# Two stacked transformer blocks in fp32 pairs: feed-forwards 2 to 4 with another split of the second product, other banks for two units, and two plain products

## Chip, cores and metric

One core of one Trainium2 chip runs the whole kernel. The metric is the device time of one execution in microseconds (us). All inputs and outputs are fp32. The kernel has four feed-forwards (FF), one in each of its four layers; the change touches the last three of them.

## The reference, cut to what matters

```python
# first block, layers 0 and 1
h = rmsnorm(x, norm_ffn_g[l]) * (1.0 + sc2) + sh2
f = (jax.nn.silu(h @ ffn_w1[l]) * (h @ ffn_w3[l])) @ ffn_w2[l]
x = x + g2 * f
...
# second block, layers 0 and 1
gate, up = jnp.split(x @ w_ffn_in[i], 2, axis=-1)
ffn = (jax.nn.silu(gate) * up) @ w_ffn_out[i]
ple = (p[i] @ w_ple[i]) * jax.nn.sigmoid(x @ w_ple_gate[i])
x = layer_norm(ALPHA * x + ffn + ple, ln2_g[i], ln2_b[i])
```

There are 512 tokens of width 1024, and the hidden width is 2816. Attention, pooling, retention, convolution and gating stand ahead of each feed-forward and are not changed.

## The kernel before

**Number format.** Each fp32 operand is split into a high part (fp32r, made by ACT) and a low part (the rest, `raw - hi`, made by POOL or DVE). One product is three matmuls: high by low, low by high, high by high (`three`, lines 2789 to 2791).

**Pairs, units, parts.** The hidden width is 11 pairs of 2 x 128 columns. A unit is one load of weights with the products that use it. The order is written out by the class `Plan`: for each pair i one unit of the up side (`plain` or `upper`; w3, or the second half of w_ffn_in) and one of the gate side (`seven`, or `whole` for pair 0 of a feed-forward of the first block), then some `down` units. A `plain` unit has 4 parts of 12 matmuls of 512 columns. A `seven` or `upper` unit computes the same 256 hidden columns in the seven products of a Strassen-Winograd scheme: 7 parts M1, M6, M7, M5, M4, M2, M3, each of 12 matmuls of 256 columns. It needs four sums of weight quarters (`dve_sums`, lines 2062 to 2067, tile `u_sum`) and five operations on DVE that add up the results (`parts` in `dve_ffn`, lines 2095 to 2112). Every part has a slot in a ring of 8 (`k_hi`, `k_lo`). A slot is filled again when PE has done the part that held it, and the fill is three steps: ACT's high part (line 1097), the low part (line 1654 on POOL or 2047 on DVE), PE.

**Down units.** The second product (w2) is summed in PSUM over a pass of pairs and then added to x. `SPREAD` gives the passes of feed-forwards 2 to 4: pairs 0-1, 2-3, 4-5, 6-7, 8-10. Each pass has four `down` units of 256 output columns. The units of the first four passes lie between the pairs; those of the last pass are the tail, units 38 to 41. A down unit has one part of 12 matmuls of 512 columns for each pair of its pass.

**The gate.** When both units of a pair are done, ACT takes the silu (line 1121), DVE multiplies with the up side (`gated`, line 2125, tile `u_full`), ACT makes `f_hi` (line 1126) and POOL (line 1674) or DVE (line 2133) makes `f_lo`. PE takes a bank again when its reader is done (`bank_taken`); for the bank of a `plain` unit that reader is `gated`.

**Order on the engines.** All queues are in order. ACT, POOL and DVE walk through the same list of parts `t` as PE. `Plan.after[t]` says which slots are filled behind part t; `Plan.summed` says ahead of which part DVE makes the sums of a later unit. SP issues the loads in the order of the units; a load waits for the low parts of the unit that used the buffer before. In the first block SP also loads pieces of the modulation matrix (`sp_modulation_b`), and DVE weighs them (lines 1895 and 1898, tile `r`).

**The end of a feed-forward in the second block.** When the first half of unit 40 is done, PE sums x over the first four of its eight column blocks with a matmul by ones (line 3629); DVE then subtracts, adds and squares (`dve_shift_norm`, lines 2484 to 2498), and PE takes up those sums (lines 3346 and 3348) ahead of the last six matmuls of unit 41.

Of the kernel before, what the change touches and what calls it, by code (L numbers as in the profile page):

```python
# [36 lines left out]
DEPTH = 2  # L37
# [17 lines left out]

PAIRS = FF // G
PASSES = [range(0, 4), range(4, 7), range(7, PAIRS)]
SPREAD = [range(0, 2), range(2, 4), range(4, 6), range(6, 8), range(8, PAIRS)]
AHEAD = [0, 1, 0]
SPARE = 5  # L60
RING = 8
# [5 lines left out]
class Plan:  # L67
# [8 lines left out]
    def __init__(self, early, spread, uppers=(), sets=(1,)):  # L76
        self.units, self.spread, self.sets = [], spread, sets
        self.early, self.spare = early, SPARE - 1 if spread else SPARE
        self.passes = SPREAD if spread else PASSES
        downs = [("down", n, j) for n in range(len(self.passes)) for j in range(KD // 2)]  # L80
        upto = {pairs[-1] + AHEAD[n]: KD // 2 for n, pairs in enumerate(PASSES)}
        if spread:
            upto = {i: 4 if early and i == 3 else 2 for i in range(3 if early else 2, PAIRS - 1)}
        for i in range(PAIRS):
            self.units += [("upper" if i in uppers else "plain", i, 0),
                           ("whole" if early and i == 0 else "seven", i, 0)]
            self.units += downs[:upto.get(i, 0)]
            del downs[:upto.get(i, 0)]
        self.units += downs
        self.tail = len(self.units) - KD // 2  # L90
        self.seq = [(u, n) for u in range(len(self.units)) for n in range(self.count(u))]
        self.at = {x: q for q, x in enumerate(self.seq)}
        self.slot, self.before, holds = [], [], {}
        for q, (u, n) in enumerate(self.seq):
            k = LAST_SLOTS[u - self.tail][n] if u >= self.tail else q % RING
            self.slot.append(k)
            self.before.append(holds.get(k, -1))
            holds[k] = q
        self.after, at = {t: [] for t in range(len(self.seq))}, 0
        for q in range(RING, len(self.seq)):  # L100
            at = max(at, self.before[q])
            self.after[at].append(q)
        self.mine = [self.on_vector(u, n) for u, n in self.seq]
        self.summed = {}
        for u, (kind, _, _) in enumerate(self.units):
            if kind in SEVENS and self.at[u, M6] >= RING:
                t = next(t for t, qs in self.after.items() if self.at[u, M6] in qs)
                self.summed[t - (3 if spread and (kind == "upper" or len(sets) > 1) else 1)] = u
        self.source, self.loads, self.old, used = [], [], [], {}
        for u in range(len(self.units)):  # L110
            x = self.buffer(u)
            self.source.append(x)
            self.loads.append(sum(y == x for y in self.source))
            self.old.append(used.get(x))
            used[x] = u
# [17 lines left out]
    def banks(self, u):  # L133
        kind, i, j = self.units[u]
        if kind == "seven":
            return 0, 4, 1, 5
        if kind == "upper":
            return 2, 6, 3, 7
        if kind == "whole":
            first = 0  # L140
        elif kind == "plain":
            late = i > 0 and (i != 2 or not self.early)
            first = 6 if (late if self.spread else (i % 2 == 1) != (i >= len(PASSES[0]))) else 2
        else:
            first = 2 * (u % 2) if not self.spread or u >= self.tail else 0 if j % 2 else 2
        return first, first + 1

    def pair_units(self, i):
# [23 lines left out]
        return self.mine[q], sum(m == self.mine[q] for m in self.mine[:q + 1])  # L172


PLAN = [Plan(True, False), Plan(True, True, range(4, PAIRS))] + [Plan(False, True, range(1, PAIRS), (2, 1))] * DEPTH
UNITS = {1: 10 + 4, 2: 9 + 4 + 5}
UNIT0 = {1: 0, 2: DEPTH * UNITS[1]}

# [286 lines left out]
class Sems:  # L465

    def __init__(self, nc, ctx):
# [89 lines left out]
        def by_plan(name, count):  # L557
            return FfnSignal(ctx.enter_context(nc.semaphore(name)), [count(p) for p in PLAN])

# [327 lines left out]
def sp_layer1(sp, e, l, more):  # L887
    a, b, s = e.a, e.b, e.s
    lay = Layer(s, 1, l)

    def units(js):
        for j in js:
            sp_weights(sp, e, lay, j, a["w_in"], l, IN1[UNIT_COLS1[j]])

    if l == 0:
        units((2, 3))
        sp.wait_ge(*s.mod(l, 1))
        sp_gains(sp, e, (0, 1, 2, 3))
        units((4,))
        sp_gains(sp, e, (4, 5))  # L900
        units((5,))
        sp_gains(sp, e, (6, 7))
        sp.wait_ge(s.z_ready.up, 9 + Z_COPIES)
    else:
        sp_after_ffn(sp, e, l - 1)
        units((0, 1))
        sp.wait_ge(*s.f_x(l - 1, KD * len(PLAN[l - 1].passes)))
        sp.wait_ge(*s.r(l * 2, 2))
    sp.dma_start(b.decay[:, :, :], a["decay"]).then_inc(s.decay_in.up, 16)
    for m in range(2):  # L910
        sp.dma_start(b.pw[:, m, :], a["pool_w"][l, 2 * m:2 * m + 2, :, :].rearrange("e c d -> (e c) d"))\
          .then_inc(s.decay_in.up, 16)
    units(range(6 if l == 0 else 2, 10))
    for j in range(4):
        sp_weights(sp, e, lay, 10 + j, a["w_out"], l, G * j)
    sp.wait_ge(*s.gn_o(l, 2))
    for n in range(4):
        sp_modulation_b(sp, e, l, n)
    ffn = a["ffn_w1"], a["ffn_w3"], 0, a["ffn_w2"], l
    for u in range(2):  # L920
        sp_ffn_unit(sp, e, lay, u, *ffn)
    sp.wait_ge(*s.hl(l * 2 + 1, 1))
    for n in (4, 5):
        sp_modulation_b(sp, e, l, n)

    def between(u):
        if u in (4, 6):
            sp_modulation_b(sp, e, l, 6 + (u - 4) // 2)
        if u == 8 and lay.plan.spread:
            sp.wait_ge(*s.b_acc(l, 3 * KD + KD // 2))  # L930
        if more and 10 <= u < 10 + A_CHUNKS:
            sp_next_modulation(sp, e, l, u - 10)

    sp_ffn(sp, e, lay, *ffn, 2, between)
    if more:
        sp_parameters(sp, e, l + 1)
# [730 lines left out]
def pool_ffn(pool, e, lay):  # L1667
    s, b, plan, n = e.s, e.b, lay.plan, lay.ffn

    def hidden(i):  # L1670
        for m in range(2):
            at = i % plan.spare * 2 + m
            pool.wait_ge(*s.fh(n, 2 * i + m + 1))
            pool.tensor_tensor(b.f_lo[:, at, :], b.f_full[:, m, :], b.f_hi[:, at, :].bitcast(F32), ALU.subtract)\
                .then_inc(s.fl.up, 1)

    for t, (u, part) in enumerate(plan.seq):
        if part == 1 and plan.gate_done(u) is not None and not plan.hidden_on_vector(u):
            hidden(plan.gate_done(u))
        for q in plan.after[t]:  # L1680
            pool_low(pool, e, lay, q)
# [2024 lines left out]
```

## Time and profile before

| | before |
|---|---|
| median of 3 runs | 2558.11 us (2552.84 to 2560.55) |
| the profiled execution | 2559.09 us |
| its span in the profile | 2557.3 us |
| mean granted TensorE clock | 0.979 of full speed |
| feed-forwards 2, 3, 4 in the span | about 895 to 1234, 1527 to 1884, 2177 to 2533 us |

The profile shows one execution. Its span lacks 1.8 us that lie around it. Times in the rows are from the start of the span; "PE" is TensorE, "DVE" VectorE, "ACT" ScalarE, "POOL" GpSimd.

### The profile page before, as it was taken

Reading aid. Unit: us, or ns where it says so; the run is one execution under the profiler, and the core shown is the slowest. Engines: PE = TensorE matmul, PEld = TensorE weight load, DVE = VectorE, ACT = ScalarE, POOL = GpSimd, SP = SyncE. Lnnn points to the kernel's source line nnn. Section 1 sums busy time; section 2 is a strip of 40 time slices with the busy share of each in tenths; the row PEclk is TensorE's granted clock in tenths of the full one; section 3 lists DMA queues with packets and bytes.
Section 4 is the critical chain, followed back from the end, with each engine's and each line's share of the span. In section 5 each row is a group of like instructions: output and inputs, shape, how many; then the busy total and the mean of one; then the engine's idle time right before and its main releaser. Section 6 shows DMA issues by size and latency. Waiting matters only on the chain.

```text
span 2557.3 us, 35757 instructions
## 1 busy us (share of the span) xinstructions
PE 2442.4 (96%) x13831; PEld 2055.3 (80%) x13831; DVE 1841.5 (72%) x2737; ACT 1109.2 (43%) x1827; POOL 1080.9 (42%) x606
## 2 busy tenths in 40 slices
PE   7999999999999999999899998999989999899997
PEld 4776788888776788998677778999967777899995
DVE  5686777854487796776686477888668747888876
ACT  4335443323425443444443554444444355444442
POOL 0332462524324353545153456445514534655541
PEclk8999999999999999999999999999999999999998
DMA  8514346543222433332331223333223212333321
GB/s 281 199 50 132 116 142 193 188 137 101 85 82 83 132 116 116 100 107 76 100 83 58 67 66 108 108 99 100 83 80 83 75 50 66 99 104 112 107 79 46
DMA packets 239650, 268.92 MB, mean 105 GB/s; under 512 B 19977, under 2 KB 204025, under 8 KB 239225
## 3 DMA queue, kind: packets, MB, share of 16 engines
q1 hardware_dynamic: 239480, 266.63, 32.3%
q8 instruction: 110, 1.80, 0.3%
q14 instruction: 60, 0.48, 0.1%
HBM read 264.51 MB, written 2.10 MB: 104 GB/s over the span
## 4 chain that ended last, share of the span: by engine, by line
PE 74%; DVE 11%; issue 4%; ACT 4%; DMA 3%; POOL 3%; SPq 0%; ACTq 0%; DVEq 0%; POOLq 0%
PE bank L2789 22%; PE bank L2791 22%; PE bank L2790 22%; DVE r L1898 2%; DVE m_cv L2239 2%; POOL w_lo L1643 1%; DMA raw<-in_ffn_w 1%; DVE k_lo L2047 1%; POOL k_lo L1654 1%; DMA raw<-in_w_ffn_in 1%; PE bank L3423 1%; DMA b_raw<-in_ada_w 1%; ACT w_hi L1043 1%; ACT k_hi L1097 1%; PE bank L3456 1%
## 5 line engine op out<-in xcount | busy, mean ns | idle before, releaser
L1654 POOL TENSOR_TENSOR k_lo<-raw,k_hi 128x512 fp32r<-128x512 f32 x303 | 440.3, 1462 | 569.4 <-ACT k_hi L1097 568.6
L1643 POOL TENSOR_TENSOR w_lo<-raw,w_hi 128x2048 fp32r<-128x2048 f32 x53 | 248.5, 4688 | 532.4 <-ACT w_hi L1043 457.5
L1097 ACT ACTIVATE k_hi<-raw 128x512 fp32r<-128x512 f32 x432 | 265.0, 626 | 310.3 <-PE bank L2791 244.1
L2789 PE MATMUL bank<-h_hi,k_lo 128*128 128x256 f32 (+1 forms) x1132 | 355.6, 314 | 17.4 <-DVE u_full L2125 13.7
L2790 PE MATMUL bank<-h_lo,k_hi 128*128 128x256 f32 (+1 forms) x1132 | 354.2, 313 | 0.0
L2791 PE MATMUL bank<-h_hi,k_hi 128*128 128x256 f32 (+1 forms) x1132 | 354.1, 313 | 0.0
L2789 PE MATMUL bank<-h_hi,w_lo 128*128 128x512 f32 x800 | 325.2, 406 | 8.6 <-DVE h_lo L2007 3.9
L2791 PE MATMUL bank<-h_hi,w_hi 128*128 128x512 f32 x800 | 314.0, 393 | 0.0
L2790 PE MATMUL bank<-h_lo,w_hi 128*128 128x512 f32 x800 | 313.7, 392 | 0.0
L2791 PE MATMUL bank<-u_t_hi,k_hi 128*128 128x256 f32 x1104 | 310.9, 282 | 0.0
L2789 PE MATMUL bank<-u_t_hi,k_lo 128*128 128x256 f32 x1104 | 310.3, 281 | 0.0
L2790 PE MATMUL bank<-u_t_lo,k_hi 128*128 128x256 f32 x1104 | 307.9, 279 | 0.0
L2789 PE MATMUL bank<-f_hi,k_lo 128*128 128x512 f32 x704 | 279.7, 397 | 10.5 <-DVE x L2393 4.5
L2790 PE MATMUL bank<-f_lo,k_hi 128*128 128x512 f32 x704 | 275.8, 392 | 0.0
L2791 PE MATMUL bank<-f_hi,k_hi 128*128 128x512 f32 x704 | 275.5, 391 | 0.0
L2789 PEld LDWEIGHTS bank<-h_hi,k_lo 128*128 128x128 f32 x1132 | 216.9, 192 | 32.8 <-DVE u_full L2125 14.1
L2790 PEld LDWEIGHTS bank<-h_lo,k_hi 128*128 128x128 f32 x1132 | 217.3, 192 | 12.5
L2791 PEld LDWEIGHTS bank<-h_hi,k_hi 128*128 128x128 f32 x1132 | 217.3, 192 | 12.0
L1097 ACT ACTIVATE k_hi<-u_sum 128x512 fp32r<-128x512 f32 x207 | 129.9, 628 | 184.4 <-PE bank L2791 123.0
L2789 PEld LDWEIGHTS bank<-u_t_hi,k_lo 128*128 128x128 f32 x1104 | 209.0, 189 | 0.0
L2790 PEld LDWEIGHTS bank<-u_t_lo,k_hi 128*128 128x128 f32 x1104 | 208.8, 189 | 0.0
L2791 PEld LDWEIGHTS bank<-u_t_hi,k_hi 128*128 128x128 f32 x1104 | 208.0, 188 | 0.0
(401 smaller groups left out, 5013.0 us busy)
## 6 DMA issues: line engine op xcount, KB each, us to landing
raw<-in_ffn_w SPq DMA_DIRECT2D x52, 1024.0 KB, 5.4
raw<-in_w_ffn_in SPq DMA_DIRECT2D x44, 1024.0 KB, 5.1
raw<-in_w_in SPq DMA_DIRECT2D x34, 1024.0 KB
b_raw<-in_ada_w SPq DMA_DIRECT2D x32, 1024.0 KB, 5.2
f_raw<-in_w_ffn_out SPq DMA_DIRECT2D x32, 512.0 KB, 3.4
z_a<-in_ada_w SPq DMA_DIRECT2D x4, 2048.0 KB, 14.1
g_raw<-in_ada_w SPq DMA_DIRECT2D x8, 1024.0 KB, 5.4
raw<-in_w_out SPq DMA_DIRECT2D x8, 1024.0 KB
```

The costliest lines, as they stand in the source:

```text
L1043: act.activation(b.w_hi[p][:, 0:n], b.raw[p][:, 0:n], ACT.Copy).then_inc(s.hi.up, 1)
L1097: act.activation(hi, src, ACT.Copy).then_inc(s.f_hi.up, 1)
L1643: pool.tensor_tensor(b.w_lo[p][:, 0:n], b.raw[p][:, 0:n], b.w_hi[p][:, 0:n].bitcast(F32), ALU.subtract)\
L1654: pool.tensor_tensor(lo, src, hi.bitcast(F32), ALU.subtract).then_inc(s.f_lo.up, 1)
L1898: dve.scalar_tensor_tensor(acc, raw[:, k - ks[0], :], c[:, k:k + 1], acc, ALU.mult, ALU.add)\
L2047: dve.tensor_tensor(lo, src, hi.bitcast(F32), ALU.subtract).then_inc(s.f_lod.up, 1)
L2239: dve.scalar_tensor_tensor(b.cv[:, m, :], b.ch[:, m, t:t + T], b.taps[:, n:n + 1], b.cv[:, m, :], ALU.mult, ALU.add).then_inc(s.conv.up, 1)
L2789: pe.matmul(out, wlo, xhi, start=start, stop=False)
L2790: pe.matmul(out, whi, xlo, start=False, stop=False)
L2791: return pe.matmul(out, whi, xhi, start=False, stop=stop)
L3423: op = pe.matmul(bank[at][:, c:c + n], b.n_q[o:o + HD, p, i * P:(i + 1) * P], b.n_k[o:o + HD, p // 2, 0:n], start=False, stop=(h, i) in (( ...
L3456: op = pe.matmul(bank[5][HD * h:HD * (h + 1), j * P:T], b.n_v[:, j, v], b.n_probT[h][:, KEY_AT[j]:KEY_AT[j] + T - j * P], start=(j == 0), ...
```

## The change

`SPREAD` becomes passes of 2, 2, 2, 1 and 4 pairs: pair 7 moves from the fourth pass to the tail. Units 30, 31, 34 and 35 have one part in place of two, units 38 to 41 have four in place of three. The up side of pairs 9 and 10 is a `plain` unit (2 units in each of three feed-forwards). In feed-forwards 3 and 4 the first unit, which is plain, writes banks 3 and 7 in place of 2 and 3; in feed-forward 2 the third down unit (unit 10) writes banks 6 and 7 in place of 2 and 3. In feed-forwards 3 and 4 DVE makes the sums of units 3 and 5 three parts later. In feed-forward 2 SP issues the last modulation piece behind the load of unit 7 in place of unit 6. POOL makes `f_lo` at a down unit's only part where it has just one.

```diff
-SPREAD = [range(0, 2), range(2, 4), range(4, 6), range(6, 8), range(8, PAIRS)]
+SPREAD = [range(0, 2), range(2, 4), range(4, 6), range(6, 7), range(7, PAIRS)]
...
-                self.summed[t - (3 if spread and (kind == "upper" or len(sets) > 1) else 1)] = u
+                ahead = 3 if spread and (kind == "upper" or len(sets) > 1) else 1
+                if len(sets) > 1 and kind == "seven" and self.units[u - 2][0] == "seven":
+                    ahead = 0
+                self.summed[t - ahead] = u
...
+            if self.spread and self.early and i == 0 and j == 2:
+                first = 6
+        if kind == "plain" and self.spread and not self.early and i == 0:
+            return 3, 7
         return first, first + 1
...
-PLAN = [Plan(True, False), Plan(True, True, range(4, PAIRS))] + [Plan(False, True, range(1, PAIRS), (2, 1))] * DEPTH
+PLAN = [Plan(True, False), Plan(True, True, range(4, 9))] + [Plan(False, True, range(1, 9), (2, 1))] * DEPTH
...
-        if u in (4, 6):
+        if u in (4, 7 if lay.plan.spread else 6):
...
-        if part == 1 and plan.gate_done(u) is not None and not plan.hidden_on_vector(u):
+        if part == min(1, plan.count(u) - 1) and plan.gate_done(u) is not None and not plan.hidden_on_vector(u):
```

The file of the change has seven lines more, so line 2062 of before is line 2069 of the change, and so on.

**DVE at the start of feed-forward 3**, before, from part M4 of unit 1 on; `u_act<-u_third,bank` to `u_act<-u_row,bank` are that unit's results, `u_sum_116` to `118` the sums of unit 3:

```order
L2105 TENSOR_TENSOR u_act<-u_third,bank 128x512
L2108 TENSOR_TENSOR u_row<-u_row,bank 128x256
L2062 TENSOR_TENSOR u_sum_116<-raw_53 128x512
L2064 TENSOR_TENSOR u_sum_117<-u_sum_116,raw_53 128x512
L2065 TENSOR_TENSOR raw_53<-raw_53 128x4x128
L2067 TENSOR_TENSOR u_sum_118<-raw_53,u_sum_117 128x512
L2047 TENSOR_TENSOR k_lo<-raw_52,k_hi 128x512
L2112 TENSOR_TENSOR u_act<-u_row,bank 128x512
L2047 TENSOR_TENSOR k_lo<-u_sum_108,k_hi 128x512
L2125 TENSOR_TENSOR u_full<-u_act,bank 128x512 x2
```

and the same place in the change:

```order
L2112 TENSOR_TENSOR u_act<-u_third,bank 128x512
L2115 TENSOR_TENSOR u_row<-u_row,bank 128x256
L2054 TENSOR_TENSOR k_lo<-raw_52,k_hi 128x512
L2119 TENSOR_TENSOR u_act<-u_row,bank 128x512
L2054 TENSOR_TENSOR k_lo<-u_sum_108,k_hi 128x512
L2132 TENSOR_TENSOR u_full<-u_act,bank 128x512 x2
L2069 TENSOR_TENSOR u_sum_116<-raw_53 128x512
L2071 TENSOR_TENSOR u_sum_117<-u_sum_116,raw_53 128x512
L2072 TENSOR_TENSOR raw_53<-raw_53 128x4x128
L2074 TENSOR_TENSOR u_sum_118<-raw_53,u_sum_117 128x512
```

The four sums of unit 3 stood ahead of the last result of unit 1 and of the gate of pair 0; now they stand behind them.

**PE at the same place**, before: the end of unit 1 (bank 5) and the beginning of unit 2. `f_gated` is the signal of the gate's multiplication:

```order
L2789 MATMUL bank5<-h_hi_50,k_lo_120 128x256
L2790 MATMUL bank5<-h_lo_51,k_hi_119 128x256
L2791 MATMUL bank5<-h_hi_50,k_hi_119 128x256
L2789 MATMUL bank2<-h_hi_50,k_lo_120 128x256 [waits f_lo,f_gated]
L2790 MATMUL bank2<-h_lo_51,k_hi_119 128x256
```

and the place in unit 2 where the change first waits for that signal, from part M7 (bank 6) to part M5 (bank 3):

```order
L2797 MATMUL bank6<-u_t_lo_115,k_hi_119 128x256
L2798 MATMUL bank6<-u_t_hi_113,k_hi_119 128x256
L2796 MATMUL bank3<-u_t_hi_113,k_lo_120 128x256 [waits f_lod,f_gated]
L2797 MATMUL bank3<-u_t_lo_115,k_hi_119 128x256
L2798 MATMUL bank3<-u_t_hi_113,k_hi_119 128x256
```

The wait for the gate of pair 0 moved from the first part of unit 2 to its fourth, 36 matmuls later.

**ACT at the end of feed-forward 2**, before, from the first sum of unit 37 (`u_row<-bank`) on; `raw_52` and `raw_53` hold the weights of units 38 and 39, and the second `u_act` is the silu that the gate of pair 10 waits for:

```order
L1116 ACTIVATE u_row<-bank 128x256
L1097 ACTIVATE k_hi<-raw_52 128x512
L1121 ACTIVATE u_act<-u_act 128x512
L1097 ACTIVATE k_hi<-raw_52 128x512 x2
L1097 ACTIVATE k_hi<-raw_53 128x512 x3
L1121 ACTIVATE u_act<-u_act 128x512
L1126 ACTIVATE f_hi<-u_full 128x512 x2
```

and in the change:

```order
L1123 ACTIVATE u_row<-bank 128x256
L1128 ACTIVATE u_act<-u_act 128x512
L1104 ACTIVATE k_hi<-raw_52 128x512 x4
L1104 ACTIVATE k_hi<-raw_53 128x512 x4
L1128 ACTIVATE u_act<-u_act 128x512
L1133 ACTIVATE f_hi<-u_full 128x512 x2
```

In the change all eight high parts of units 38 and 39 stand behind the end of unit 37: the first slot of unit 38 is the slot of unit 37's last part (both are slot 0 in the ring of 8), and `after` never lets a later slot be filled ahead of an earlier one. In feed-forwards 3 and 4 the slots fall otherwise: units 37's last part holds slot 4, and the four high parts of unit 38 lie ahead of its end, those of unit 39 behind it.

## Rows read from the trace of the kernel before

**Rows 1.** The page, parts 1 and 5: busy time by engine; the largest group on POOL

```profile
PE 2442.4 (96%) x13831; PEld 2055.3 (80%) x13831; DVE 1841.5 (72%) x2737; ACT 1109.2 (43%) x1827; POOL 1080.9 (42%) x606
...
L1654 POOL TENSOR_TENSOR k_lo<-raw,k_hi 128x512 fp32r<-128x512 f32 x303 | 440.3, 1462 | 569.4 <-ACT k_hi L1097 568.6
```

**Rows 2.** Timeline of PE, feed-forward 2: starts of units 12, 13, 14, 16

```profile
991.89 0.28 PE L2789 MATMUL bank<-h_hi,k_lo 128*128 128x256 f32 x1
...
1001.86 0.28 PE L2789 MATMUL bank<-h_hi,k_lo 128*128 128x256 f32 x1
...
1011.83 0.40 PE L2789 MATMUL bank<-f_hi,k_lo 128*128 128x512 f32 x1
...
1022.74 0.28 PE L2789 MATMUL bank<-h_hi,k_lo 128*128 128x256 f32 x1
```

**Rows 3.** Timeline of PE and DVE around the start of unit 10, feed-forward 2

```profile
974.51 0.39 PE L2791 MATMUL bank<-f_hi,k_hi 128*128 128x512 f32 x1
979.40 0.76 PE L2789 MATMUL bank<-f_hi,k_lo 128*128 128x512 f32 x1 [4.50 <-DVE x L2393]
...
971.91 0.69 DVE L2062 TENSOR_TENSOR u_sum<-raw 128x512 f32<-128x512 f32 x1 [3.91 <-DMA raw<-in_ffn_w]
...
975.90 1.29 DVE L2125 TENSOR_TENSOR u_full<-u_act,bank 128x512 f32<-128x512 f32 x2 [0.76 <-ACT u_act L1121]
...
977.89 1.41 DVE L2393 SCALAR_TENSOR_TENSOR x<-bank,mod,x 128x512 f32<-128x512 f32 x2
```

**Rows 4.** Timeline of PE and ACT, unit 38 of feed-forward 2; last, feed-forward 1

```profile
1202.15 0.39 PE L2791 MATMUL bank<-f_hi,k_hi 128*128 128x512 f32 x1
1205.05 0.77 PE L2789 MATMUL bank<-f_hi,k_lo 128*128 128x512 f32 x1 [2.50 <-DVE f_lo L2133]
...
1197.11 2.20 ACT L1097 ACTIVATE k_hi<-raw 128x512 fp32r<-128x512 f32 x4 [0.81 <-PE bank L2791]
...
362.85 0.47 PE L2789 MATMUL bank<-f_hi,k_lo 128*128 128x512 f32 x1 [2.43 <-DVE u_row L2108]
```

**Rows 5.** Timeline of four engines, start of feed-forward 3

```profile
1547.94 0.28 PE L2791 MATMUL bank<-h_hi,k_hi 128*128 128x256 f32 x1
1555.37 0.58 PE L2789 MATMUL bank<-h_hi,k_lo 128*128 128x256 f32 x1 [7.15 <-DVE u_full L2125]
...
1567.21 0.28 PE L2789 MATMUL bank<-h_hi,k_lo 128*128 128x256 f32 x1
...
1549.10 0.63 ACT L1097 ACTIVATE k_hi<-raw 128x512 fp32r<-128x512 f32 x1 [1.65 <-DMA raw<-in_w_ffn_in]
...
1553.25 0.68 DVE L2112 TENSOR_TENSOR u_act<-u_row,bank 128x512 f32<-128x512 f32 x1
...
1554.63 1.28 DVE L2125 TENSOR_TENSOR u_full<-u_act,bank 128x512 f32<-128x512 f32 x2
...
1566.51 1.66 DVE L2064 TENSOR_TENSOR u_sum<-u_sum,raw 128x512 f32<-128x512 f32 x1
...
1561.32 3.35 POOL L1674 TENSOR_TENSOR f_lo<-u_full,f_hi 128x512 fp32r<-128x512 f32 x2 [9.73 <-ACT f_hi L1126]
```

**Rows 6.** Timeline of PE, start of feed-forward 4

```profile
2197.72 0.28 PE L2791 MATMUL bank<-h_hi,k_hi 128*128 128x256 f32 x1
2204.53 0.58 PE L2789 MATMUL bank<-h_hi,k_lo 128*128 128x256 f32 x1 [6.54 <-DVE u_full L2125]
```

**Rows 7.** Timeline of PE and DVE, tail of feed-forward 3

```profile
1864.33 1.02 PE L3629 MATMUL bank<-r,ones 128*128 128x512 f32 x2
...
1879.23 1.13 PE L3346 MATMUL bank<-r,ones 128*128 128x512 f32 x2 [2.96 <-DVE r L2493]
...
1883.97 0.40 PE L2791 MATMUL bank<-f_hi,k_hi 128*128 128x512 f32 x1
...
1865.38 4.87 DVE L2498 SCALAR_TENSOR_TENSOR x<-bank,x 128x512 f32<-128x512 f32 x8 [2.39 <-PE bank L3629]
...
1878.48 0.69 DVE L2493 TENSOR_TENSOR r<-r,x 128x512 f32<-128x512 f32 x1
```

## The prediction

> **What bounds the kernel now.** The page comes first: PE is busy for 96% of the span, DVE for 72%, POOL for 42% [rows 1]. So PE's own work, and what keeps PE waiting, set the time; work on another engine counts only where PE waits for it. The second view is the timeline of PE through feed-forwards 2 to 4. Between the pairs it has no holes: a `seven` or `upper` unit of 84 matmuls takes 1001.86 - 991.89 = 9.97 us, and 48 matmuls of 512 columns take 1022.74 - 1011.83 = 10.91 us, 0.227 us each [rows 2]. So an 84-matmul unit has parts of 1.42 us, a down or plain part takes 2.73 us, and a `plain` unit 10.91 us. Third come the places where PE does stop. In these three feed-forwards there are six that matter, in four kinds:
>
> (a) Feed-forward 2, unit 10. PE ends unit 9 at 974.51 + 0.23 = 974.74 and starts again at 979.40, 4.66 us later, when DVE has emptied banks 2 and 3 (977.89 + 1.41 = 979.30). DVE is late because it stood 3.91 us for a load and then had sums and a gate to do [rows 3]. The first matmul afterwards takes 0.76 us, not 0.39: the granted clock is at 1.2 GHz, its lower level. The 48 matmuls up to 991.89 [rows 2] take 12.49 us, 1.6 more than 10.91. Loss 6.3 us.
>
> (b) Feed-forward 2, unit 38. After 24 matmuls PE waits for `f_lo` of pair 10: 1205.05 - 1202.38 = 2.67 us, and again the clock falls (0.77 us) [rows 4]; with the same 1.6 us the loss is 4.3 us.
>
> (c) Feed-forwards 3 and 4, unit 2. It wants bank 2, which the plain unit 0 left full until the gate of pair 0. In feed-forward 3 that is 1555.37 - 1548.06 = 7.31 us, and the unit's 84 matmuls then take 1567.21 - 1555.37 = 11.84 us, 1.87 more than 9.97 [rows 2, 5]. Loss 9.2 us. In feed-forward 4: 2204.53 - 2197.84 = 6.69 us [rows 6], with the same 1.87 us 8.6 us.
>
> (d) The tails of feed-forwards 3 and 4. From the half of unit 40 (1864.33) to the end of unit 41 (1883.97 + 0.23) 19.87 us pass. PE has 54 matmuls to do there, 12.26 us, and three matmuls by ones at no more than 1.02 us each, 3.06. The loss is 4.6 us: PE waits until 1879.23 for DVE's sum `r`, and DVE works from 1865.38 on without a rest [rows 7]. I take the same for feed-forward 4.
>
> **The change, part by part.**
>
> *Plain units for pairs 9 and 10.* Six units go from 9.97 to 10.91 us of PE: 0.94 x 6 = 5.6 us more, 1.9 in each feed-forward. PE is the bound between the pairs, so nothing hides this. DVE and POOL lose work there (four sums, five results, three low parts a unit), which earns nothing by itself.
>
> *Pair 7 to the tail.* PE's work is the same; four units lose 12 matmuls and four gain them. What it buys is cover. In (d), DVE has `r` ready at 1878.48 + 0.69 = 1879.17, 14.84 us after the half of unit 40 [rows 7]. The change gives PE 24 + 24 + 18 = 66 matmuls there ahead of the sums, 14.98 us, and one matmul by ones: 15.8 to 16.0 us. That covers DVE by about 1 us, and the squares come one short DVE operation later, behind another matmul by ones. So the 4.6 us go, in each of two feed-forwards. The least it can give is 3.1: the 12 extra matmuls of unit 41 and a little.
> In (b) PE gets 36 matmuls (8.2 us) in place of 24 ahead of pair 10. But the order of ACT in the change shows a new hole: unit 38 can't get its first slot before unit 37 has ended. ACT's high part (0.55, a quarter of 2.20 [rows 4]), POOL's low part (1.46 [rows 1]) and the hand-overs (0.2 before ACT, as in [rows 4]) give 2.3 us of idle PE. Eight high parts in place of four put off the silu by 2.2 us, so `f_lo` comes at 1205.0 + 2.2 = 1207.2, 10.3 us after unit 37's end (1196.9), while PE wants it at 2.3 + 8.2 = 10.5. No second wait. Loss 2.3 in place of 4.3 if the clock holds: gain 2.0. The clock is the unknown: after 2.43 us of idle it held (0.47 us), after 2.50 it fell (0.77) [rows 4]. At 2.3 I take it as holding; the other end is a gain of 0.4.
>
> *Unit 10 in banks 6 and 7.* It must wait for the gate of pair 3 instead, which is done at 975.90 + 1.29 = 977.19, not 979.30 [rows 3]: gain 2.1 us. The idle time falls from 4.50 to 2.4, nearest to the row where the clock held, so I add the 1.6 us: 3.7. The other end is 2.1. What is late next is the gate itself, behind the load that lands for DVE at 971.91; unit 12 takes banks 2 and 6 far later.
>
> *The first plain unit in banks 3 and 7, sums later.* Unit 2 wants bank 3 first at its fourth part, 4.27 us after it starts, at 1552.3. The gate of pair 0 was at 1554.63 + 1.28 because DVE had done the four sums of unit 3 first and only then the last result of unit 1 (1553.25) [rows 5]. With the sums behind, DVE has that result by 1549. ACT still stands at the high part of unit 3 for a load, until 1549.10 + 0.63 = 1549.73 [rows 5]; the silu ends at 1550.4, the two products at 1551.7. That is ahead of 1552.3, so the hole of (c) goes: 9.2 and 8.6 us. PE then runs 9 us earlier against DVE, and something else can be late. Sums of unit 3: 1551.7 to 1554.4 or so, wanted by PE at 1548.06 + 9.97 + 1.42 = 1559.5; fine. Next, DVE's result of M4 of unit 2 waits for `f_lo` of pair 0; ACT makes the high parts by about 1556, POOL needs 3.35 us [rows 5], so 1559.3; only then come the sums of unit 4 (2.7 us at 0.68 each, 4.7 if half of them take 1.66 [rows 5]), and the low part of M2 of unit 3 at 1562.7 to 1565. PE wants it at 1565.1. Pair 2 repeats this with the moved sums of unit 5. I put 1.8 us of new waits on each feed-forward; the ends are 0 and 4.
>
> By the Trainium skill (SBUF — State Buffer, SBUF: two separate sides), a DVE operation with two SBUF inputs and a GpSimd operation that reads SBUF exclude each other for a whole instruction. The sum at 1566.51, 1.66 us in place of 0.68, agrees. By that rule all four sums behind the gate could take 1.66, 6.6 us, which would put the low part of M2 at 1566.6 and add some 1.5 us a feed-forward: this is part of the second rival.
>
> *The modulation piece.* SP's load of unit 7 waits for low parts anyway, the piece is weighed some 20 us later, and `f_lo` of pair 9 at a one-part unit costs the same. I cost these at nothing; if the piece came late, DVE would hold up the emptying of banks, at most the few us of (a) again.
>
> **The sum.** Feed-forward 2: 3.7 + 2.0 - 1.9 = 3.8. Feed-forward 3: 9.2 - 1.8 + 4.6 - 1.9 = 10.1. Feed-forward 4: 8.6 - 1.8 + 4.6 - 1.9 = 9.5. Together 23.4 us off 2559.1, the profiled execution's own time (1 us above the median of the runs shown): 2535.7, say 2536 us.
>
> **The rivals.**
> *DVE becomes the bound at the starts (0.18).* For it: the moved sums meet POOL's `f_lo` and low parts, and DVE has 9 us less time. Against it: the slack of 4 us at unit 3's sums worked out above. Each of feed-forwards 3 and 4 then keeps 3 to 5 us of the hole, with 1.87 us of slow clock if it is one long wait: 10 us less gain, 2546 us.
> *The tails give nothing (0.06).* If DVE's chain there hangs on something later than the half of unit 40, for instance on ACT with two more high parts a unit, it shifts with PE. For it: DVE rests between units 38 and 40. Against it: its start at 1865.38 is released by PE's line 3629 [rows 7]. 2536 + 9 = 2545 us.
> *The bank changes don't do what they say (0.05).* If a load, not a bank, sets (a) and (c), only 4.27 us of (c) are covered by the three parts moved ahead: 2559.1 less 2 x (4.27 - 1.9 + 4.6) - 1.9 gives 2547 us.
> *Slower (0.04).* The sums of units 3 and 5 stand behind the gate. If they came so late that PE waited at the second part of those units, each us late costs PE a us, twice. It decides at 11.7 us late in each of two feed-forwards, that is sums of unit 3 ready only near 1571; at 15.6 us late the time is 2567 us. Only a load of unit 3 or POOL far behind could do it, and the load lands at 1549.
> *The forecast (0.67)* holds 2531 to 2541: 2531 with no new waits at all, 2541 with the clock falling at both places and 3 us of new waits in each start.
>
> **Range and chances.** A difference of 0.3% (7.7 us) is about what a measurement of this kernel tells from no change. Faster by more takes all cases down to 2550: 0.93. Same 0.04, slower 0.03. The range of 8 in 10 reaches from just under the best case, 2529, to the rivals at 2546 to 2547: 2529 to 2547.
>
> **What would show it.** In the profile after: unit 2 of feed-forwards 3 and 4 starts within 0.2 us of unit 1's end, and DVE's `u_full` product stands ahead of the sums from `raw`; PE's wait for `r` at line 3353 is gone; unit 10 starts some 2 us earlier; PE has a hole of 2.3 us for `k_lo` at the start of unit 38 in feed-forward 2. I would be wrong if PE showed new waits for `k_lo` on DVE in pairs 1 and 2, or if units 32 to 37 had holes because loads come too late for the shorter pairs.

## The result, and the profile after

The change makes the kernel 1.1% faster. Its median is 2528.71 us (2523.63 to 2535.36, 4 runs) against 2556.59 us for the kernel before (4 runs): a ratio of 0.9892 [0.9864, 0.9921]. Two later measurements of the same change gave 0.9887 [0.9874, 0.9901] and 0.9902 [0.9886, 0.9919]. The forecast was 2536, in a range from 2529 to 2547: the time fell just under its lower end, and the gain is some 25 to 28 us where 23.4 were worked out.

The busy times of the page, which answer to [rows 1]:

```profile
PE 2440.2 (96%) x13615; PEld 2044.6 (81%) x13615; DVE 1771.5 (70%) x2671; ACT 1094.8 (43%) x1803; POOL 1067.2 (42%) x600
```

PE's busy time is nearly what it was: the saving is idle time. The view of windows puts it in its place. Each row is a stretch, its length, and the busy us of PE, PEld, DVE, ACT and POOL, then the granted clock and the DMA. Of before, feed-forwards 2 and 3 (the first window begins 1.9 us behind the start of its feed-forward):

```profile
877.70:1234.40 356.70, 348.60 (x2207) 316.03 (x2206) 265.64 (x350) 153.86 (x262) 164.80 (x104) 0.99 0.35 109
1527.20:1884.20 357.00, 346.89 (x2347) 320.98 (x2345) 280.20 (x376) 157.89 (x268) 179.79 (x117) 0.99 0.31 97
```

and of after:

```profile
875.80:1233.80 358.00, 352.05 (x2140) 315.52 (x2141) 249.37 (x330) 151.56 (x256) 160.25 (x102) 0.99 0.34 109
1525.60:1871.00 345.40, 344.65 (x2274) 316.58 (x2274) 255.47 (x354) 152.27 (x260) 174.24 (x115) 1.00 0.32 101
```

In feed-forward 3 PE is now idle for 0.75 us in all, where it was 10.1, with the clock at full, and feed-forward 4 is the same; feed-forward 2 has gained nothing. Counted from the start of the first to the start of the last matmul of a feed-forward, in us (the kernels e2 to e13 are described under Experiments):

| kernel | FF2 | FF3 | FF4 |
|---|---|---|---|
| before, three profiled executions | 357.6, 357.7, 356.5 | 356.8, 356.8, 356.8 | 355.7, 356.1, 356.1 |
| the change, three | 358.0, 356.6, 358.5 | 345.4, 345.7, 345.5 | 345.4, 345.2, 345.2 |
| e2_passes | 353.4 | 359.7 | 358.8 |
| e3_starts | 356.7 | 349.3 | 350.0 |
| e5_banks37 | 357.7 | 351.2 | 353.1 |
| e6_sums | 356.6 | 350.5 | 350.6 |
| e4_uppers | 349.7 | 350.5 | 350.0 |
| e13_upper_banks | 351.5 | 347.7 | 345.4 |
| e10_ff2_upper | 352.5 | 345.2 | 346.5 |
| e12_nine_upper | 349.6 | 344.5 | 344.3 |

The three feed-forwards are 21.6 us shorter on the mean of three runs each (1070.1 against 1048.5).

**The starts of feed-forwards 3 and 4.** PE and DVE in feed-forward 3, which answer to [rows 5]:

```profile
1547.81 0.28 PE L2798 MATMUL bank<-h_hi,k_hi 128*128 128x256 f32 x1
1547.93 0.28 PE L2796 MATMUL bank<-u_t_hi,k_lo 128*128 128x256 f32 x1
...
1579.15 0.28 PE L2798 MATMUL bank<-u_t_hi,k_hi 128*128 128x256 f32 x1
1580.18 0.36 PE L2796 MATMUL bank<-u_t_hi,k_lo 128*128 128x256 f32 x1 [0.75 <-POOL k_lo L1661]
```
```profile
1548.65 1.28 DVE L2132 TENSOR_TENSOR u_full<-u_act,bank 128x512 f32<-128x512 f32 x2 [0.67 <-ACT u_act L1128]
1549.85 0.68 DVE L2069 TENSOR_TENSOR u_sum<-raw 128x512 f32<-128x512 f32 x1
...
1558.11 1.67 DVE L2071 TENSOR_TENSOR u_sum<-u_sum,raw 128x512 f32<-128x512 f32 x1
```

Unit 2 follows unit 1 without a gap; the gate stands ahead of the sums and starts 6.0 us earlier than before, of which 1.6 are the earlier start of the whole feed-forward. One new wait is left, 0.9 us for a low part of POOL (1580.18 less 1579.15 and the usual 0.12).

**The tails.** PE, which answers to [rows 7]:

```profile
1852.28 1.02 PE L3636 MATMUL bank<-r,ones 128*128 128x512 f32 x2
...
1868.15 1.02 PE L3353 MATMUL bank<-r,ones 128*128 128x512 f32 x2
...
1871.02 0.40 PE L2798 MATMUL bank<-f_hi,k_hi 128*128 128x512 f32 x1
```
```profile
1866.44 0.69 DVE L2500 TENSOR_TENSOR r<-r,x 128x512 f32<-128x512 f32 x1
```

From the half of unit 40 to the end 1871.25 - 1852.28 = 18.97 us pass, for 72 matmuls (16.34) and the ones; before it was 19.87 for 54. The time beyond the 512-column matmuls of the products is 7.61 us before and 2.63 us now, so the loss is 4.98 us less. DVE has `r` ready at 1867.13, 1.0 us before PE asks: the cover that was forecast ("about 1 us").

**Feed-forward 2, units 10 and 38.** PE, which answers to [rows 3, 4]:

```profile
974.45 0.39 PE L2798 MATMUL bank<-f_hi,k_hi 128*128 128x512 f32 x1
977.26 0.47 PE L2796 MATMUL bank<-f_hi,k_lo 128*128 128x512 f32 x1 [2.42 <-DVE u_full L2132]
...
978.43 0.63 PE L2797 MATMUL bank<-f_lo,k_hi 128*128 128x512 f32 x1
978.86 0.63 PE L2798 MATMUL bank<-f_hi,k_hi 128*128 128x512 f32 x1
...
1186.18 0.28 PE L2798 MATMUL bank<-h_hi,k_hi 128*128 128x256 f32 x1
1188.73 0.47 PE L2796 MATMUL bank<-f_hi,k_lo 128*128 128x512 f32 x1 [2.27 <-POOL k_lo L1661]
...
1190.19 0.63 PE L2798 MATMUL bank<-f_hi,k_hi 128*128 128x512 f32 x1
```

In this execution both holes have the length that was worked out (2.4 and 2.3 us of idle PE). The one at unit 38 has it in all three profiled executions of the change; the one at unit 10 was longer in the two others (by the starts 2.85 and 3.54 us, where it is 2.58 here). But look at the rows behind the holes: 1.2 and 1.5 us after PE starts again a matmul takes 0.63 us in place of 0.39, and the next comes 0.43 us later in place of 0.23. The granted clock fell to 1.2 GHz after both holes, where it was taken as holding. That the first matmul behind a hole takes only 0.47 us, which the prediction read as a clock that holds, is no sign of it here. And this feed-forward also pays 1.9 us for its two plain units (2 x 0.94): its matmuls without holes and slow stretches take 347.1 us, before 345.3.

### The profile page after: what moved, and what is told of

It reads as the page before. It is cut to its first block, busy times and chain, and to the rows that moved or that the text cites. A ratio compares the mean times of both kernels' runs of the same rounds, so it can differ in the third digit from the quotient of the medians.

```text
span 2533.6 us, 35157 instructions
## 1 busy us (share of the span) xinstructions
PE 2440.2 (96%) x13615; PEld 2044.6 (81%) x13615; DVE 1771.5 (70%) x2671; ACT 1094.8 (43%) x1803; POOL 1067.2 (42%) x600
## 4 chain that ended last, share of the span: by engine, by line
PE 71%; DVE 12%; issue 5%; ACT 4%; POOL 4%; DMA 3%; SPq 0%; ACTq 0%; DVEq 0%; POOLq 0%
PE bank L2796 21%; PE bank L2798 21%; PE bank L2797 21%; DVE r L1905 2%; DVE m_cv L2246 2%; DVE k_lo L2054 1%; DMA raw<-in_ffn_w 1%; DMA raw<-in_w_ffn_in 1%; POOL w_lo L1650 1%; POOL k_lo L1661 1%; PE bank L3430 1%; DVE u_sum L2071 1%; ACT k_hi L1104 1%; DMA b_raw<-in_ada_w 1%; ACT w_hi L1050 1%
## 5 line engine op out<-in xcount | busy, mean ns | idle before, releaser
L2796 PE MATMUL bank<-h_hi,k_lo 128*128 128x256 f32 (+1 forms) x1156 | 371.4, 321 | 3.8 <-DVE k_lo L2054 2.5
L2797 PE MATMUL bank<-h_lo,k_hi 128*128 128x256 f32 (+1 forms) x1156 | 370.2, 320 | 0.0
L2798 PE MATMUL bank<-h_hi,k_hi 128*128 128x256 f32 (+1 forms) x1156 | 370.0, 320 | 0.0
L2796 PE MATMUL bank<-u_t_hi,k_lo 128*128 128x256 f32 x1008 | 282.9, 281 | 1.5 <-POOL k_lo L1661 1.5
L2798 PE MATMUL bank<-u_t_hi,k_hi 128*128 128x256 f32 x1008 | 283.5, 281 | 0.0
L2797 PE MATMUL bank<-u_t_lo,k_hi 128*128 128x256 f32 x1008 | 280.7, 278 | 0.0
L2796 PEld LDWEIGHTS bank<-h_hi,w_lo 128*128 128x128 f32 x800 | 151.2, 189 | 57.6 <-issue 19.4
L1104 ACT ACTIVATE k_hi<-u_sum 128x512 fp32r<-128x512 f32 x189 | 118.6, 627 | 177.7 <-PE bank L2798 100.0
L2796 PEld LDWEIGHTS bank<-u_t_hi,k_lo 128*128 128x128 f32 x1008 | 190.1, 189 | 1.9 <-DVE u_row L2115 1.9
L2797 PEld LDWEIGHTS bank<-u_t_lo,k_hi 128*128 128x128 f32 x1008 | 190.0, 189 | 0.0
```

The source lines that it names most:

```text
L1104: act.activation(hi, src, ACT.Copy).then_inc(s.f_hi.up, 1)
L2796: pe.matmul(out, wlo, xhi, start=start, stop=False)
L2797: pe.matmul(out, whi, xlo, start=False, stop=False)
L2798: return pe.matmul(out, whi, xhi, start=False, stop=stop)
```

## Experiments

The kernels e2, e3, e5 and e6 are the kernel before with the lines shown, and they also keep two small edits of the change: the later modulation piece in feed-forward 2, and POOL's line for down units of one part, which alters nothing where every down unit has two. Feed-forward 2 takes 356.7, 357.7 and 356.6 us in e3, e5 and e6, and 356.5 to 357.7 us before: the move of the modulation piece shows neither cost nor gain.

**The change again, twice** (e1_again, e14_change_third), and the kernel before again, twice (e11_before_again, e15_before_third), to tell apart what is chance in a single profile. e1_again: 

> The change itself once more, for a second profile and more times. Theory A (the sum over stages is right, 23 to 24 us off, and single executions differ by how long the granted clock is at its lower level): the median lies 22 to 28 us below before; between single runs, 0.001 of mean granted clock goes with 2 to 3 us; stages ahead of feed-forward 2, which the change does not touch, differ between two profiles by some us in either direction. Theory B (the change also gives something outside the six places): the stages outside feed-forwards 2 to 4 are shorter than before in both profiles.


e14_change_third: 

> The change, for a third profile and a direct comparison with the next kernel. Feed-forwards 2, 3, 4 at 357, 345.5 and 345.3 us as in its two profiles; ratio to before 0.989.


e11_before_again: 

> The kernel before once more, for a second profile. Theory A (the 4 to 6 us by which the medians moved more than the feed-forwards is chance of the granted clock in stages that no edit touches): the stages outside feed-forwards 2 to 4 sum to 1105 to 1111 us as in the profiles of the change and of the parts, not 1113 us as in the first profile of before; feed-forwards 2 to 4 as in the first profile within 2 us each. Rival (something of the change reaches those stages): 1113 us again.


e15_before_third: 

> The kernel before, for a third profile. The same two theories, 1105 to 1111 us or 1113 us outside the feed-forwards 2 to 4 (feed-forward 1 left out too).

Measured: e1_again 2531.27 us, 0.9887 [0.9874, 0.9901]; e14_change_third 2528.32 us, 0.9902 [0.9886, 0.9919]; single runs of before 2555.64 and 2553.54. The lengths of feed-forwards 3 and 4 repeat within 0.4 us, that of feed-forward 2 within 2 us: the clock fell after both holes in the first profile, after one in each of the others. Outside the four feed-forwards the executions of before spend 1113.3, 1108.0 and 1106.9 us, those of the change 1110.8, 1108.2 and 1101.9. So the 1113 us of the first profile of before was chance, as e11_before_again expected, and the stages there can differ by 2 to 6 us from run to run without an edit.

**The passes alone.**

```diff
 # in the kernel before
-SPREAD = [range(0, 2), range(2, 4), range(4, 6), range(6, 8), range(8, PAIRS)]
+SPREAD = [range(0, 2), range(2, 4), range(4, 6), range(6, 7), range(7, PAIRS)]
```

> Passes 2, 2, 2, 1, 4 alone, on before: up sides of pairs 9 and 10, banks and sums as before. Theory A (cover in the tails): each tail of feed-forwards 3 and 4 gives 4.6 to 5 us, unit 38 of feed-forward 2 4.3 us (no hole at its start, since its slots come free early here): 13 to 14 us off before. Rival (with 7-part up sides DVE can't keep pace with the shorter pairs 9 and 10, which is what the plain units are for): holes of some us in units 32 to 37, 5 to 9 us off.

Measured: 2553.59 us, 0.9983 [0.9972, 0.9994]. This is far from the 13 to 14 us of theory A. Feed-forward 2 is 3.9 us shorter, but feed-forwards 3 and 4 each got 3 us longer. The waits of PE in feed-forward 3 (us in total, times, longest):

```profile
PE bank L2790 <- DVE u_full L2126: 7.3, 1, 7.3
PE bank L2790 <- DVE x L2756: 2.3, 2, 1.2
PE bank L2790 <- DVE f_lo L2134: 2.1, 1, 2.1
```

The tail's wait for `r` is gone, as forecast, but two waits for a bank and one for `f_lo` are new, in each of feed-forwards 3 and 4: 4.9 us of holes and 1.6 us of slow clock behind the last, against the 5.0 us that the tail saves. About 1 us more of slow clock behind the old hole at unit 2 of feed-forward 3 comes on top. The rival's holes came, though their cause turns out to be banks and slots (below). The first, at the start of unit 32, on PE and on DVE:

```profile
1780.83 0.39 PE L2792 MATMUL bank<-f_hi,k_hi 128*128 128x512 f32 x1
1782.38 0.39 PE L2790 MATMUL bank<-h_hi,k_lo 128*128 128x256 f32 x1 [1.16 <-DVE x L2756]
```
```profile
1776.93 1.66 DVE L2063 TENSOR_TENSOR u_sum<-raw 128x512 f32<-128x512 f32 x1
...
1779.83 0.68 DVE L2068 TENSOR_TENSOR u_sum<-raw,u_sum 128x512 f32<-128x512 f32 x1
1780.43 1.28 DVE L2126 TENSOR_TENSOR u_full<-u_act,u_full 128x512 f32<-128x512 f32 x2
1781.63 1.28 DVE L2756 TENSOR_TENSOR x<-bank,x 128x512 f32<-128x512 f32 x2
```

With one part in place of two, down unit 30 lasts 2.7 us. DVE, behind its sums and the gate, adds it to x only at 1781.63, and the `upper` unit 32 wants bank 2 first.

**The starts alone.** The kernel before with the lines for unit 0's banks and for the later sums of units 3 and 5.

```diff
 # in the kernel before
+                if len(sets) > 1 and kind == "seven" and self.units[u - 2][0] == "seven":
+                    ahead = 0
...
+        if kind == "plain" and self.spread and not self.early and i == 0:
+            return 3, 7
```

> Banks 3 and 7 for unit 0 and the later sums of units 3 and 5 in feed-forwards 3 and 4 alone, on before. Theory A: the holes of 7.3 and 6.7 us and the slow clock behind them go, less a wait of about 1 us behind them each: 15 to 16 us off. Rival (DVE bound at the starts): 8 us off.

Measured: 2544.22 us, 0.9942 [0.9929, 0.9955], 15.1 us by the medians, as theory A had it; feed-forwards 3 and 4 are 7.5 and 6.0 us shorter than before, the tails' waits stay. So the start edits carry 13.5 us of the 21.6 by themselves, and they don't hang on the new passes.

**Its two halves.** e5_banks37 has the banks without the later sums, e6_sums the sums without the banks.

```diff
 # e5, from e3
-                if len(sets) > 1 and kind == "seven" and self.units[u - 2][0] == "seven":
-                    ahead = 0
 # e6, from e3
-        if kind == "plain" and self.spread and not self.early and i == 0:
-            return 3, 7
```

e5_banks37: 

> Banks 3 and 7 for unit 0 of feed-forwards 3 and 4 alone, on before; the sums stay ahead of the gate. Theory A (bank wait and the order on DVE are two halves): unit 2 starts at once, and PE waits at its part M5 for the gate, which is still some 7.3 us behind unit 1's end, so 7.3 - 4.3 = 3.0 us of idle stay there in each; with both together giving 6.6 us a feed-forward on the chip, this alone gives 4 to 5.5. Rival (the bank alone is enough): as much as both, 6.6 us a feed-forward.


e6_sums: 

> The later sums of units 3 and 5 in feed-forwards 3 and 4 alone, on before; unit 0 stays in banks 2 and 3. Theory A: the gate comes some 4 us earlier (about 3.5 us behind unit 1's end in place of 7.3), so the hole at unit 2 falls to about 3 to 3.5 us: 3.5 to 5 us off in each feed-forward. Rival (the sums are not what holds the gate): no gain.

Measured: 2544.69 us, 0.9971 [0.9958, 0.9984], and 2542.6 us, 0.9957 [0.9943, 0.9971]. PE's wait at the start of feed-forward 3, of e5 and then of e6:

```profile
PE bank L2792 <- DVE u_full L2128: 2.2, 1, 2.2
```
```profile
PE bank L2792 <- DVE u_full L2128: 2.8, 1, 2.8
```

Each half alone cuts the hole of 7.2 us to under 3 and leaves the rest; the other half removes it. By the table e5_banks37 gains 5.6 and 2.9 us in feed-forwards 3 and 4, and e6_sums 6.3 and 5.4, where 4 to 5.5 and 3.5 to 5 had been expected: behind the holes of e6_sums (2.93 and 3.00 us) the clock held, behind those of e5_banks37 (2.34 and 2.94 us) it fell. The gains don't add up, because both go at one wait: one makes PE ask later, the other makes DVE done sooner.

**The change with `upper` units for pairs 9 and 10 again.**

```diff
-PLAN = [Plan(True, False), Plan(True, True, range(4, 9))] + [Plan(False, True, range(1, 9), (2, 1))] * DEPTH
+PLAN = [Plan(True, False), Plan(True, True, range(4, PAIRS))] + [Plan(False, True, range(1, PAIRS), (2, 1))] * DEPTH
```

> The change with 7-part units again on the up side of pairs 9 and 10. Theory A: PE has 5.6 us less to do, and unit 38 of feed-forward 2 gets its slots early, so its hole of 2.6 us and the slow clock behind it go: 8 to 10 us below the change. Rival (the plain units give DVE the time it needs in the short pairs): no faster than the change, with PE waiting for k_lo or the gate in units 34 to 38.

Measured: 2532.53 us, 0.9894 [0.988, 0.9907], beside 2531.27 for the change (e1_again). So the 8 to 10 us of theory A did not come. The totals are alike, but the feed-forwards are not: feed-forward 2 is 7 to 9 us shorter than with plain units, feed-forwards 3 and 4 are 4.8 us longer, by the three waits of e2_passes (1.32, 1.32 and 2.29 us of idle PE each time). Theory A was right for feed-forward 2 and the rival for the other two. The plain units are two edits with opposite signs.

**The same with other banks** for the `upper` units of pairs 9 and 10 in feed-forwards 3 and 4, so that they want bank 6 first, not bank 2:

```diff
 # from e4; banks of an upper unit
-            return 2, 6, 3, 7
+            return (6, 2, 7, 3) if i >= 9 and not self.early else (2, 6, 3, 7)
```

> 7-part up sides in pairs 9 and 10 everywhere, but in feed-forwards 3 and 4 with banks 6, 2, 7, 3 in place of 2, 6, 3, 7, so that units 32 and 36 begin in bank 6. Theory A (what the plain units buy in feed-forwards 3 and 4 is their banks 6 and 7, which the one-part down units ahead don't use): the two waits of 1.32 us for x go, the wait of 2.3 us for f_lo at unit 38 stays: feed-forwards 3 and 4 at about 347.5 us, 2.6 us below 350 each. Rival (it is DVE's work, sums and results, that is too much for the short pairs): PE waits there for k_lo or the gate instead, 350 us or more.

Measured: 2528.02 us, 0.9898 [0.9882, 0.9913]. Both waits of 1.32 us are gone from the trace, the one for `f_lo` stays:

```profile
PE bank L2796 <- DVE f_lo L2140: 2.1, 1, 2.1
```

So for the banks the plain units of feed-forwards 3 and 4 are not needed. The two feed-forwards differ, 347.7 and 345.4 us, because behind the same hole at unit 38 (2.29 and 2.30 us) the clock fell in the first and held in the second.

**Plain units only in feed-forwards 3 and 4.**

```diff
-PLAN = [Plan(True, False), Plan(True, True, range(4, 9))] + [Plan(False, True, range(1, 9), (2, 1))] * DEPTH
+PLAN = [Plan(True, False), Plan(True, True, range(4, PAIRS))] + [Plan(False, True, range(1, 9), (2, 1))] * DEPTH
```

> The change with 7-part up sides in pairs 9 and 10 of feed-forward 2 only (feed-forwards 3 and 4 as in the change). Theory A (the plain units pay in feed-forwards 3 and 4 and cost in 2, where they also spoil the order of the slots at unit 38): feed-forward 2 takes 350 us as with 7-part units in all three, feed-forwards 3 and 4 345 us each as in the change: 6 to 8 us below the change, about 2523 us. Rival (the three feed-forwards are linked, or the difference was one of single profiles): no different from the change.

Measured: 2522.61 us, 0.9881 [0.9868, 0.9895], close to the 2523 of theory A; by the ratio alone it can't be told from the change (0.9887 to 0.9902). In the profile feed-forward 2 is 352.5 us, 5.2 shorter than the mean of the change's three, and PE has no hole at unit 38. What goes with that hole, where the passes are the new ones, is how many high parts ACT has to make behind the end of unit 37, ahead of the silu. ACT's rows there: the change in feed-forward 2 and in feed-forward 3, then this kernel in feed-forward 2, then e2_passes in feed-forward 3:

```profile
1186.50 4.27 ACT L1104 ACTIVATE k_hi<-raw 128x512 fp32r<-128x512 f32 x8 [1.52 <-PE bank L2798]
1190.67 0.61 ACT L1128 ACTIVATE u_act<-u_act 128x512 f32<-128x512 f32 x1
...
1825.25 2.20 ACT L1104 ACTIVATE k_hi<-raw 128x512 fp32r<-128x512 f32 x4 [0.81 <-PE bank L2798]
1827.36 0.61 ACT L1128 ACTIVATE u_act<-u_act 128x512 f32<-128x512 f32 x1
```
```profile
1180.03 1.15 ACT L1104 ACTIVATE k_hi<-raw 128x512 fp32r<-128x512 f32 x2 [0.81 <-PE bank L2798]
1181.09 0.62 ACT L1128 ACTIVATE u_act<-u_act 128x512 f32<-128x512 f32 x1
```
```profile
1829.45 3.24 ACT L1098 ACTIVATE k_hi<-raw 128x512 fp32r<-128x512 f32 x6 [0.81 <-PE bank L2792]
1832.60 0.61 ACT L1122 ACTIVATE u_act<-u_act 128x512 f32<-128x512 f32 x1
```

Eight and six high parts go with a hole at unit 38, four and two with none. With eight, unit 38's own first part is among them, and PE stands at the unit's start for its low part; with six, PE has that part and stands later, for an `f_lo` that is late because the silu stood behind the six. (With the old passes PE has one part less to do ahead of `f_lo`, and there four high parts go with a hole too [rows 4].) The number is that of the slots in the ring of 8 which come free only with unit 37's end, and an `upper` unit's 7 parts in place of 4 turn the ring by three. The same kind of unit therefore helps in one feed-forward and hurts in the other.

**The best of these together.** `upper` for pairs 9 and 10 in feed-forward 2; in feed-forwards 3 and 4 `upper` for pair 9, in the other banks, and plain for pair 10.

```diff
-PLAN = [Plan(True, False), Plan(True, True, range(4, 9))] + [Plan(False, True, range(1, 9), (2, 1))] * DEPTH
+PLAN = [Plan(True, False), Plan(True, True, range(4, PAIRS))] + [Plan(False, True, range(1, 10), (2, 1))] * DEPTH
...
-            return 2, 6, 3, 7
+            return (6, 2, 7, 3) if i == 9 and not self.early else (2, 6, 3, 7)
```

> 7-part up sides in pairs 9 and 10 of feed-forward 2; in feed-forwards 3 and 4 pair 9 has 7 parts and begins in bank 6, pair 10 is plain, and the slots of units 38 and 39 come free early. Theory A (bank and slot order decide, the plain unit only costs PE 0.9 us): feed-forwards 3 and 4 at 344 to 345 us, feed-forward 2 at 350 to 352 us; 7 to 9 us below the change, about 1 to 2 below the kernel with plain units in both pairs of 3 and 4. Rival (DVE too slow with the sums of unit 32 in the short pair 9): PE waits there for k_lo or the gate, no better than the change by more than 6 us.

Measured: 2518.27 us (2512.18 to 2520.72, 4 runs), 0.9867 [0.9848, 0.9885], against 2528.32 for the change beside it (e14_change_third): 10 us better than the change. ACT at the end of unit 37, feed-forward 3:

```profile
1804.30 0.63 ACT L1104 ACTIVATE k_hi<-raw 128x512 fp32r<-128x512 f32 x1 [0.81 <-PE bank L2798]
1805.03 0.64 ACT L1128 ACTIVATE u_act<-u_act 128x512 f32<-128x512 f32 x1
```

One high part is behind unit 37's end, and PE has no wait there; each of these two feed-forwards saves the 0.94 us of one plain unit, and feed-forward 2 is 8.1 us shorter than the change's mean. About 1 of these 8.1 us is chance: the four kernels with this plan for feed-forward 2 take 349.6 to 352.5 us, by the length of the hole at unit 10 (2.18 to 3.50 us) and the clock behind it.

## Where the prediction was right, and where it failed

The mechanisms of the starts and the tails were right. The steps that failed are the clock at the two holes of feed-forward 2 ("At 2.3 I take it as holding"), the plain units ("earns nothing by itself"), a sum with no term for the stage behind feed-forward 2, and its base of 2559.1 us.

**The starts (c): right.** Forecast 7.4 and 6.8 us after 1.8 us of new waits. The hole is gone and only 0.9 us of new waits came (0.7 to 1.2 in the three runs of the change); e3_starts alone gained 7.5 and 6.0. The order of DVE in time was as worked out; of the four sums of unit 4 two took 1.7 and 1.8 us, and the rival of DVE as the bound did not come about. The one new wait is for a low part of POOL, and its size is partly luck: at the same place of feed-forward 4 it was 2.6 us in e3_starts and 2.1 in e4_uppers, where ACT had stood 2.8 and 2.3 us for a load ahead of it (0.9 in the change). The 1.8 us that were charged are within that spread.

**The tails (d): right.** Forecast 4.6 each, measured 4.98 in feed-forward 3, which counts PE's waits and the slow matmuls behind them. Feed-forwards 3 and 4 together gained 22.0 us, where 10.1 + 9.5 = 19.6 were forecast, the difference mostly the smaller new waits.

**Feed-forward 2: wrong, the clock and the plain units.** Forecast 3.7 + 2.0 - 1.9 = 3.8 us; measured -0.4 (357.3 to 357.7 on the means). The step that failed is "At 2.3 I take it as holding", and the same at unit 10. In the three profiled runs of the change the clock fell after four of the six holes, and once it cost 2.9 us. So (a) gave less than the other end of its bound, 2.1: the hole itself is 1.7 us shorter on the means (4.72 to 2.99), and the slow clock costs about as much as before. (b) gave about 0.2 (2.67 to 2.43), and a gate 0.2 us late at unit 36 was not foreseen.

**"Plain units ... earns nothing by itself": wrong.** The six units do cost 0.94 us each. But e4_uppers shows that in feed-forwards 3 and 4 they keep away 4.9 us of new waits which the shorter pass brings, and that in feed-forward 2 they cost 7 us on the mean of four kernels with `upper` units there (350.8 against 357.7): 1.9 of work, 2.4 of hole, its slow clock where it falls (about 1.5), 0.2 at the gate; the rest is the hole at unit 10 and the clock behind it, which cost more in the change's profiles (2.99 us of hole on the mean against 2.63). The forecast had found that hole in ACT's order, yet had charged it to the new passes; it belongs to the plain units.

**What was missed: the stage behind feed-forward 2.** The sum has no term for it. PE from the end of the feed-forward on, before and after:

```profile
1233.70 1.02 PE L2873 MATMUL bank<-u_full,ones 128*128 128x512 f32 x2
1237.21 1.13 PE L2875 MATMUL bank<-u_act,ones 128*128 128x512 f32 x2 [2.49 <-DVE u_act L1956]
1239.46 7.39 PE L2832 MATMUL bank<-eye_r 128*128 128x512 f32 x19 [1.12 <-issue]
1246.68 0.40 PE L2789 MATMUL bank<-h_hi,w_lo 128*128 128x512 f32 x1
```
```profile
1233.99 1.02 PE L2880 MATMUL bank<-u_full,ones 128*128 128x512 f32 x2
1236.15 1.12 PE L2882 MATMUL bank<-u_act,ones 128*128 128x512 f32 x2 [1.15 <-DVE u_act L1963]
1238.52 4.57 PE L2839 MATMUL bank<-eye_r 128*128 128x512 f32 x19 [1.24 <-issue]
1242.93 0.39 PE L2796 MATMUL bank<-h_hi,w_lo 128*128 128x512 f32 x1
```

The wait for DVE's last squares (`u_act`) is 1.35 us shorter, and the 19 matmuls by `eye_r` that keep PE busy take 4.57 us in place of 7.39, because the clock doesn't fall: before, the granted clock is 0.50 from 1238.7 to 1245.4; after, it is 1.00 from 1234 to 1247. POOL and DVE show why, before and after:

```profile
1232.05 4.56 POOL L1643 TENSOR_TENSOR w_lo<-raw,w_hi 128x2048 fp32r<-128x2048 f32 x1 [12.46 <-DVE u_full L1950]
...
1230.49 1.48 DVE L1950 TENSOR_TENSOR u_full<-u_full,u_act 128x512 f32<-128x512 f32 x2
...
1234.69 2.47 DVE L1956 TENSOR_TENSOR u_act<-x 128x512 f32<-128x512 f32 x1
```
```profile
1230.97 4.58 POOL L1650 TENSOR_TENSOR w_lo<-raw,w_hi 128x2048 fp32r<-128x2048 f32 x1 [16.54 <-DVE u_full L1957]
...
1234.97 1.13 DVE L1963 TENSOR_TENSOR u_act<-x 128x512 f32<-128x512 f32 x1
```

The last half of unit 41 has 24 matmuls in place of 18, so the squares of the half before it, and POOL's `w_lo` that is released by them, start 1.36 us earlier against the end of the feed-forward. DVE's square starts at the same distance from the last matmul in all 14 profiled executions, and always ends 0.55 us after POOL's operation, whether that ends early or late: it had to wait for it. By the Trainium skill (SBUF — State Buffer, SBUF: two separate sides) a DVE operation with two SBUF inputs and a GpSimd operation that reads SBUF exclude each other; these rows agree with it. No run moved POOL's operation alone, so this last link is read from the traces. From the start of the last matmul of the feed-forward to that of the next stage's first product 12.0 to 13.2 us pass in all six profiled executions with the old passes, and 9.2 in all eight with the new ones, e2_passes among them: the passes alone do it. On the means of three and three it is 3.6 us, none of them in the forecast.

**The sum.** Measured: 21.6 us in the feed-forwards and 3.6 behind feed-forward 2 give 25.2; the medians show 27.9, 28.0 and 25.2, and the three profiled executions of each kernel differ by 24.4 on the mean. The 0 to 3 us between are not explained by an edit; the four runs of the change measured first lie between 2523.63 us (granted clock 0.988) and 2535.36 (0.985), the profiled one the slowest. Against the forecast of 23.4: -4.2 in feed-forward 2, +2.4 in feed-forwards 3 and 4, +3.6 behind feed-forward 2. That 25.2 lies so near to 23.4 is luck: the term that was too large and the one that was missing nearly cancel.

**The base.** The 23.4 us were taken off 2559.1, the time of one profiled execution; the median of the four runs is 2556.59. The measured 2528.71 lies 7.0 us under the 2535.7 of the sum: 2.5 by the base, 1.8 by the terms above, and 2.7 that stay open. From the median of before the same sum gives 2533.2.

## What to carry to other kernels

When a change lengthens the work ahead of a stage boundary, follow the engines across the boundary: an operation of another engine that starts earlier there can free a third one and keep the clock up. Where slots are filled in a fixed ring, count which slots a later unit needs that come free last; the kind of a unit can be right in one stage and wrong in the next by that count alone. And cost a short hole on PE with the slow clock behind it unless rows of several runs show that it holds.

## What the runs showed of the hardware

After holes of nearly one length the granted clock sometimes fell and sometimes held. A hole here is the time between two starts in the timeline less the usual distance of 0.23 us (0.12 behind a matmul of 256 columns). At unit 10 it fell after 2.58 and 3.54 us (the change, e14_change_third), 2.50 (e13_upper_banks) and 3.50 (e10_ff2_upper), but held after 2.85 (e1_again), 2.35 (e4_uppers) and 2.18 (e12_nine_upper). At unit 38 with the old passes the hole was 2.66 or 2.67 us in all six profiled executions, and the clock fell in three of them. The shortest hole of these after which it fell is 2.29 us (e13_upper_banks, feed-forward 3), the longest after which it held 3.00 us (e6_sums, unit 2 of feed-forward 4). A fall cost 1.4 to 1.6 us mostly, and 2.9 us once (14 slow matmuls behind unit 10 in e14_change_third). So the length of the hole alone doesn't decide it here.
